# Hybrid decoder trunk: x with channels on partitions, and stationary weights with 256 moving columns in the down, output and o blocks

## The reference, cut to what matters

```python
for l in range(2):
    x = x + 0.5 * swiglu(rms_norm(x, g1), w_gate, w_up, w_down)     # q = 0, 4
    z = rms_norm(x, g2) @ w_in                                      # q = 1, 5
    x = x + concat([diff_attention(z), conformer_conv(z), short_conv(z)]) @ w_out
    x = x + cross_attention(rms_norm(x, g3), rms_norm(mem, gm)) @ xa_wo   # q = 2, 6
    x = x + 0.5 * swiglu(rms_norm(x, g4), w_gate, w_up, w_down)     # q = 3, 7
return rms_norm(x, final_norm)
# rms_norm(x, g) = x * rsqrt(mean(x * x over channels) + 1e-6) * g
# swiglu(h, wg, wu, wd) = (silu(h @ wg) * (h @ wu)) @ wd
```

## Time and profile before

| | |
|---|---|
| median of 3 runs | 1141.22 us |
| profiled execution, its own time | 1141.1 us |
| its span | 1139.3 us |
| instructions | 15680 |
| PE products | 6180 |
| weight splits on ACT, on DVE | 260 x 1475 ns, 260 x 1746 ns |
| read from HBM | 208.85 MB, 184 GB/s over the span |

### The profile page before, as it was taken

One profiled execution on the slowest core, in us unless ns is written; L12 is line 12 of the kernel. 1 busy time (PEld: TensorE's weight loads), 2 busy tenths in 40 slices (PEclk: granted clock), 3 DMA queues, 4 the chain that ended last, 5 costly groups with the idle time before them and its releaser, 6 DMA issues.

```text
span 1139.3 us, 15680 instructions
## 1 busy us (share of the span) xinstructions
PE 1131.4 (99%) x6180; PEld 976.9 (86%) x6180; DVE 857.4 (75%) x1164; ACT 647.1 (57%) x937; POOL 21.8 (2%) x63
## 2 busy tenths in 40 slices
PE   9999999999999999999999999999999999999997
PEld 8888888888889888888888888888888898888886
DVE  7877676899967686766777676669998676866765
ACT  6555556547755554544565555464577556645454
POOL 1000000000000000000000000000000000000000
PEclk9999999999999999999999999999999999999999
DMA  7966654644444366555547655544545444666561
GB/s 265 327 202 188 218 186 147 221 149 165 170 159 172 111 224 217 164 201 199 186 151 255 219 161 205 192 165 168 186 148 204 166 146 125 210 190 216 183 200 43
DMA packets 66266, 210.92 MB, mean 185 GB/s; under 512 B 5009, under 2 KB 24209, under 8 KB 61073
## 3 DMA queue, kind: packets, MB, share of 16 engines
q1 hardware_dynamic: 65216, 209.26, 54.0%
q10 hardware_dynamic: 976, 0.66, 0.2%
HBM read 208.85 MB, written 1.05 MB: 184 GB/s over the span
## 4 chain that ended last, share of the span: by engine, by line
PE 94%; DVE 4%; DVEq 1%; ACT 0%; issue 0%
PE G L1720 28%; PE G L1729 14%; PE D L1567 10%; PE D L1565 10%; PE D L1566 10%; PE G L1660 3%; PE G L1565 3%; PE G L1567 3%; PE G L1566 3%; PE D L1660 2%; DVE w_lo L1006 2%; PE G L1669 1%; DVE acc L1215 1%; PE D L1669 1%; PE D L1632 1%; DVEq L1217 1%
## 5 line engine op out<-in xcount | busy, mean ns | idle before, releaser
L1006 DVE TENSOR_TENSOR w_lo<-w_raw,w_hi 128x2048 fp32r<-128x2048 f32 (+3 forms) x260 | 452.6, 1746 | 54.8 <-ACT w_hi L595 54.0
L595 ACT ACTIVATE w_hi<-w_raw 128x2048 fp32r<-128x2048 f32 (+3 forms) x260 | 381.1, 1475 | 35.2 <-PE D L1567 17.0
L1720 PE MATMUL G<-a,w_hi 128*128 128x512 f32 x1406 | 346.3, 391 | 0.1
L1720 PEld LDWEIGHTS G<-a,w_hi 128*128 128x128 f32 x1406 | 256.1, 188 | 48.6 <-issue 1.1
L1729 PEld LDWEIGHTS G<-a,w_lo 128*128 128x128 f32 x1406 | 175.4, 188 | 8.6
L1729 PE MATMUL G<-a,w_lo 128*128 128x256 f32 x1406 | 177.5, 277 | 0.0
L1111 DVE TENSOR_TENSOR zqk<-G,zqk 128x512 f32<-128x512 f32 x88 | 60.8, 691 | 127.3 <-ACT zqk L674 123.3
L1565 PE MATMUL D<-w_hi,hT_hi 128*128 128x512 f32 x352 | 137.2, 390 | 0.0
L1567 PE MATMUL D<-w_hi,hT_lo 128*128 128x512 f32 x352 | 137.0, 389 | 0.0
L1566 PE MATMUL D<-w_lo,hT_hi 128*128 128x512 f32 x352 | 136.9, 389 | 0.0
L674 ACT ACTIVATE zqk<-G 128x512 f32<-128x512 f32 x88 | 52.2, 593 | 143.1 <-PE G L1729 143.1
(11 more groups left out here) (261 smaller groups left out, 1282.5 us busy)
## 6 DMA issues: line engine op xcount, KB each, us to landing
w_raw<-w_dram SPq DMA_DIRECT2D x120, 1024.0 KB, 5.0
w_raw<-w_dram SPq DMA_DIRECT2D x143, 512.0 KB, 5.3
m_raw<-memT_dram SPq DMA_DIRECT2D x2, 1024.0 KB, 8.8
w_raw<-w_dram SPq DMA_DIRECT2D x6, 256.0 KB, 6.5
w_raw<-w_dram SPq DMA_DIRECT2D x8, 128.0 KB, 3.8
vx<-mem_dram SPq DMA_DIRECT2D x1, 1024.0 KB, 10.8
x<-x_dram SPq DMA_DIRECT2D x2, 256.0 KB, 5.7
gbc<-fin_dram SPq DMA_DIRECT2D x1, 512.0 KB, 6.6
```

The source lines that it names most:

```text
L595: A(w_hi[:, part(i)], w_raw[:, part(i)], ACT.Copy).then_inc(s_hi, 1)
L1006: V.tensor_tensor(w_lo[:, part_lo(i)], w_raw[:, part(i)], w_hi[:, part(i)].bitcast(F32), ALU.subtract).then_inc(s_lo, 1)
L1720: last = M(banks[b], whi[:, at:at + P], both, start=k == 0 and not low_first, stop=k == KD - 1 and low_first, skip_group_check=low_first)
```

## The change

x is kept with channels on partitions ([128, 8, 256]), so that it needs no transposes ahead of a norm; the first norm's transposes stay, and their result is copied from PSUM to x by ACT. Down blocks (but those of the last FFN), `out` and `o` take the weights as stationary operand, 128 output channels at a time, and move 256 tokens: 24 products of 256 columns where there were 12 of 512. In FFNs the down pair of the odd chunks 5 to 19 stands between the chunk's low and high products; in the last FFN (`rows`) products and order stay as they were, and x is added in PSUM by 16 float32 products with 2·identity, so the final norm reads PSUM (with eps times 4). The sum of squares over channels is now over partitions: ACT squares, DVE adds (`channel_squares`), PE sums over partitions by two float32 products of one column, ACT copies the result for POOL. rinv_broadcast moves to the middle of chunk 2. The last block's banks are updated one by one (s_bank). Sizes and paddings of a, b, hT, m, kx and vx in memory change, and LINE goes from 128 to 64 elements.

```diff
+OFF = 48
+TURN = 16
...
-LINE = 128
+LINE = 64
...
-        x = sb("x", [P, TT, D])
-        a = sb("a", [P, KD, 2, T], F32R)
+        x = sb("x", [P, KD, T])
+        a_room = sb("a", [P, 2 * KD * T + OFF], F32R)
...
+        a, a_hi, a_lo = activations(0)
+        b, b_hi, b_lo = activations(OFF)
+        hT_room = sb("hT", [P, 2 * SLOTS_H * T + TURN], F32R)
...
+        hT_hi, hT_lo = hidden_places(0)
+        rows_hT = hidden_places(TURN)
...
-        hT_hi = sb("hT_hi", [P, SLOTS_H, T], F32R)
-        hT_lo = sb("hT_lo", [P, SLOTS_H, T], F32R)
+        sb("line_const", [P, 32])
...
-                squares(q, 1)
-                a_hi_part(q, range(4, 8))
+                to = norm_place(q)[0]
+                def high(j):
+                    act.wait_ge(s_xup, 4 * (q - 1) + j + 1)
+                    for k in (2 * j, 2 * j + 1):
+                        A(to[:, k, :], x[:, k, :], ACT.Copy, scale=gain(NORMS[q % 4], k)).then_inc(s_ahi, 1)
+                def squares(j):
+                    A(squared[j // 2][:, j % 2, :], x[:, 2 * j:2 * j + 2, :].rearrange("p k t -> p (k t)"), ACT.Square,
+                      scale=D ** -0.5).then_inc(s_sq, 1)
+                high(0)
+                high(1)
+                squares(0)
+                high(2)
+                squares(1)
+                high(3)
+                squares(2)
+                squares(3)
+            def mean_squares(q):
+                act.wait_ge(s_stat, q)
+                A(mean_sq[:, :], STAT_BANKS[q % 4][:, 0:TT], ACT.Copy).then_inc(s_ssq, 1)
+            def copy_first_x(banks):
+                act.wait_ge(s_alo, KD)
+                for j in banks:
+                    A(x[:, j::4, :], pair(DB[j]), ACT.Copy).then_inc(s_xcopy, 1)
...
                     norm_start(4 * l + 3 * f)
                     split(l, stage, ("gu", 2, 0, 8))
                     split(l, stage, ("gu", 3, 0, 8))
+                    mean_squares(4 * l + 3 * f)
                     copy_tail(l, f, 0)
                     broadcast(l, f)
...
+            def low_part(q, k):
+                hi, lo = norm_place(q)
+                dve.wait_ge(s_ahi, 8 * q + k + 1)
+                V.scalar_tensor_tensor(lo[:, k, :], x[:, k, :] if q else first_x(k), gain(NORMS[q % 4], k),
+                                       hi[:, k, :].bitcast(F32), ALU.mult, ALU.subtract).then_inc(s_alo, 1)
+            def x_update(q, j):
+                if j < 3:
+                    dve.wait_ge(s_bank, 3 * q + j + 1)
+                else:
+                    dve.wait_ge(s_blk, last_of(q // 4, LAST_STAGES[q % 4]) + 1)
+                xs = x[:, 2 * j:2 * j + 2, :]
+                V.scalar_tensor_tensor(xs, pair(DB[j]), FACTORS[q % 4], xs, ALU.mult, ALU.add).then_inc(s_xup, 1)
             def norm_lo(q):
-                a_lo_part(q, range(0, 2))
-                second_half(q - 1)
-                a_lo_part(q, range(2, 8))
+                x_update(q - 1, 1)
+                for k in range(0, 2):
+                    low_part(q, k)
+                x_update(q - 1, 2)
+                for k in range(2, 4):
+                    low_part(q, k)
+                x_update(q - 1, 3)
+                for k in range(4, 8):
+                    low_part(q, k)
+            def channel_squares(q):
+                dve.wait_ge(s_sq, 4 * q)
+                V.tensor_tensor(v_sb[:, :, :], v_sb[:, :, :], gbc[:, :, :], ALU.add)
+                dve.drain()
+                V.tensor_tensor(v_sb[:, 1, :], v_sb[:, 0, :], v_sb[:, 1, :], ALU.add)
+                dve.drain()
+                V.tensor_tensor(channel_sum, v_sb[:, 1, 0:T], v_sb[:, 1, T:], ALU.add).then_inc(s_chsum, 1)
...
                 else:
                     norm_lo(4 * l + 3 * f)
+                    channel_squares(4 * l + 3 * f)
+                    split(l, stage, ("gu", 2, 0, 8))
+                    if 4 * l + 3 * f == 4 * L - 1:
+                        twice_identity()
                     rinv_diag(l, f)
-                    split(l, stage, ("gu", 2, 0, 8))
                     pair_sum(l, f, 0)
                     split(l, stage, ("gu", 3, 0, 8))
                     pair_scale(l, f, 0)
...
-                return V.tensor_tensor(y[:, t, w], x[:, t, w], fing[:, w], ALU.mult)
+                dve.wait_ge(s_sqr, 2 * t + n + 1)
+                return V.tensor_tensor(y[:, t, w], DB[2 * n + t][:, :], fing[:, w], ALU.mult)
...
+            def channel_products(d, hi, lo, whi, wlo, n, k, start, stop):
+                w = slice(n * D + d * P, n * D + (d + 1) * P)
+                M(channels(d), whi[:, w], hi[:, k, :], start=start and d % 2 == 0, stop=False, skip_group_check=True)
+                M(channels(d), whi[:, w], lo[:, k, :], start=False, stop=False, skip_group_check=True)
+                return M(channels(d), wlo[:, w], hi[:, k, :], start=False, stop=stop, skip_group_check=True)
...
+            def last_down(q, hi, lo, ks):
+                whi, wlo = weights(last_of(q // 4, LAST_STAGES[q % 4]))
+                for d in range(KD):
+                    for n, k in enumerate(ks):
+                        last = channel_products(d, hi, lo, whi, wlo, n, k, False, n == 1)
+                    if d in (1, 3, 5):
+                        last.then_inc(s_bank, 1)
                 last.then_inc(s_blk, 1)
...
+            def residual_by_token():
+                pe.wait_ge(s_twice, 1)
+                pe.wait_ge(s_ssq, 4 * L)
+                for k in range(KD):
+                    for t in range(TT):
+                        M(DB[2 * (k // 4) + t][:, k % 4 * P:(k % 4 + 1) * P], x[:, k, tok(t)], twice,
+                          start=k % 4 == 0, stop=False, skip_group_check=True)
...
+            def mean_squares(q):
+                pe.wait_ge(s_chsum, q)
+                for t in range(TT):
+                    last = M(STAT_BANKS[q % 4][:, t:t + 1], channel_sum[:, tok(t)], ones[:, 0:1], start=t == 0, stop=True,
+                             skip_group_check=True)
+                last.then_inc(s_stat, 1)
...
                     for k in range(0, KD, 2):
-                        if k == 2:
-                            second_transposes(q)
+                        if k == 6:
+                            mean_squares(q)
...
+                def down_chunk(c, done):
                     pe.wait_ge(s_hlo, chunk(l, f, c))
-                def down_chunk(c):
-                    hidden_ready(c)
-                    down(l, stage, ("down", c), hT_hi, hT_lo, (c % SLOTS_H,), c == 0)
+                    if (q, c) == (0, 0):
+                        pe.wait_ge(s_xcopy, 4)
+                    if rows:
+                        token_down(l, stage, ("down", c), *rows_hT, c % SLOTS_H)
+                    else:
+                        down(l, stage, ("down", c), hT_hi, hT_lo, (c % SLOTS_H,), c == 0, done=done)
+                def down_pair(c, done=1):
+                    down_chunk(c, done)
+                    down_chunk(c + 1, done)
                 for c in range(2, STEPS):
                     pe.wait_ge(s_sum, chunk(l, f, c - 2))
-                    for ks in late_parts(l, f, c):
-                        gate_up(l, f, c, range(*ks), low_first=ks[0] == 2 if (q, c) == (0, 2) else c % 2 == 1)
-                        if (q, c, ks) == (0, 2, (0, 2)):
-                            rinv_broadcast()
-                    if c % 2 and c < STEPS - 2:
-                        down_chunk(c - 3)
-                        down_chunk(c - 2)
-                down_chunk(STEPS - 4)
-                down_chunk(STEPS - 3)
-                hidden_ready(LAST)
+                    early = c % 2 and 3 < c < STEPS - 2 and not rows
+                    if c % 2 == 0:
+                        for ks in late_parts(l, f, c):
+                            gate_up(l, f, c, range(*ks), low_first=ks[0] == 2 if (q, c) == (0, 2) else False,
+                                    middle=rinv_broadcast if q and c == 2 else None)
+                            if (q, c, ks) == (0, 2, (0, 2)):
+                                rinv_broadcast()
+                    else:
+                        for ks in late_parts(l, f, c):
+                            gate_up(l, f, c, range(*ks), low_first=True, between=(lambda: down_pair(c - 3, 0)) if early else None)
+                    if c == 3 and rows:
+                        residual_by_token()
+                    if c % 2 and c < STEPS - 2 and not early:
+                        down_pair(c - 3)
+                down_pair(STEPS - 4)
+                pe.wait_ge(s_hlo, chunk(l, f, LAST))
                 ks = ((STEPS - 2) % SLOTS_H, LAST % SLOTS_H)
-                if q < 4 * L - 1:
+                if not rows:
                     last_down(q, hT_hi, hT_lo, ks)
                     return
                 whi, wlo = weights(last_of(l, stage))
                 for t, at, end in ENDS:
-                    c = at // N
                     for n, k in enumerate(ks):
-                        w = slice(n * D + at, n * D + end)
```

(54 more changed lines are left out.)

264 lines of the change are left out of this document (128 added, 136 removed).

## The result

The changed kernel takes 1146.66 us (median of 6 runs, 1146.26 to 1146.93), the kernel before 1140.74 in the runs beside it: ratio 1.0049, 95% interval 1.0036 to 1.0062. It is slower by half a per cent, where the forecast was 1138.0, a gain of 3. The profiled execution took 1146.93, its span is 1145.2.

The account below looks back on a forecast made before the run. PE, busy 99%, was taken to bound the kernel. Gains of 13.2 us less costs of 10.2 gave net 3.0 us off the profiled 1141.1, say 1138.0 us; range 1134 to 1145.5.

Parts of the forecast that it names:

- part 1: Down, out and o: 1176 products become 2352 at 113.3 ns, some at 117.5; costs 2.0 us plus 0.3 for row changes.
- Rival B: Slower: 256-column products with changing weights cost 117.5 or 119.8 ns wherever they stand; 1146 or 1151 us; chance 0.11.
- rival A: Faster: nothing slow behind 512-column products and no wait for pair_sum; 3.8 us more gained, 1134.3 us; chance 0.15.
- Rival E: Each product costs something beside its columns; 1176 added ones cost 2.6 us, 1140.6, no change; chance 0.03.
- part 2: Seven norms: two blocks of 8 transposes each go, 0.87 us per block, 12.2 us gained over 14 blocks.
- part of 3: PE's added float32 work: mean_squares in seven norms costs 2.1 us, residual_by_token between FFN blocks 3.6 us.
- part 6: Ends and cross attention: start 0.4 us late, end 0.5 gained, the 64-byte distance in cross gains 0.5.
- part 4: Norm's serial path into an FFN: PE waits 0.6 us for pair_sum, 1.8 over three FFNs; mixer and cross 0.
- part 5: Steady FFN pairs: low weights of the odd block are ready 0.5 us before PE needs them; cost 0.
- Rival C: Slower: the steady pairs' 0.5 us cover is missing, PE waits for low weights; 1145 at 0.3 per pair; chance 0.08.

Follow-up runs that it names:

- p7: Changed kernel with the first two high products of the odd chunk put between its 16 low products and the early downs; 1141.53 us.
- p8: p5 with all places of 64 and 0 modulo 128 exchanged, for moving and stationary operands; 1151.0 us.
- p11: Kernel before the change, with even chunks in plain order: 16 high, then 16 low products, without the inserted 2 low and 2 high; 1145.36 us.
- p5: Changed kernel with hT and b at 0 modulo 128 and both w_hi and w_lo of the turned blocks at 64; 1141.37 us.
- p4: Changed kernel with a at 64 modulo 128 and no SHIFT, giving low products the places of the turned ones; 1145.8 us.
- p3: Changed kernel with two channel blocks of different banks taking turns in most down, out and o blocks, places in memory unchanged; 1146.9 us.
- p9: p5 with mean_squares earlier and, at c = 21 and c = 3, two down products ahead of the odd chunk's last two high ones; 1139.89 us.
- p12: p9 with DVE's low split of the next stage's fourth block moved behind the third update of x; 1138.80 us.
- p2: Changed kernel with hT and b at 0 modulo 128, w_hi and the turned blocks' w_lo at 64; 1157.7 us.

## Why the prediction was wrong, step by step

- **Turned products (part 1), the step that failed.** The prediction said: "all three new products have the 64-byte distance. So I take 113.3 as the ground rate", and "the pairs at c = 5 to 19 follow 30 low products, where the rate is 113.3". Both facts about the places hold. The conclusion doesn't: an equal distance was taken to be enough for the low row's 113.3 to hold in the downs behind it, though every fast row that had been seen lay at (0, 64). p7, p8 and p11 show that the rate hangs on the products before, p5 and p4 that downs keep a low row's 113.3 when their places are that row's own. In the changed kernel they are exchanged, (0, 64) to (64, 0), and 2203 of 2352 turned products ran between 116 and 122 ns. The term measured 9.1 in place of 2.3 us. Its bound, "all 2352, 9.9 us", was right and was then left out of the range.
- **Rival B** had the size ("At 117.5 everywhere ... 1146") and the wrong reason: neither a price of the product nor the triple's order (p3). What spoke against it, the row of 30 at 113.3, was one half of the truth. The sentence "16 products held 117.5 to the last", written against rival A, was the other half: a carried-over rate. So B's 1146 came near by luck of the size, not by its mechanism.
- **Rival E.** The Trainium skill's "TensorE: Matmul & The Clock Gate" (Back-to-back issue gap) gives an isolated warm product N/2.4 + 2.5 ns, by which two halves would cost 2.5 ns more than a whole, an estimate. The traces don't agree: two halves cost 0 ns more (5.44 us for 48 in p5 and for 24 before) or 9 (5.65 in the changed kernel), so there is no one surcharge.
- **Transposes and residual (part 2 and part of 3)** came as worked out: 11.1 and 1.2 of late starts behind them against 12.2, and 3.49 with 0.09 behind it against 3.6. **mean_squares** did not come cheaper by its single column: three of its four passes take 0.11 us, like those of 128 columns. It is 0.36 and 0.09 of late start against 0.3, so 3.2 us for seven against 2.1.
- **The 64-byte distance in cross attention (part 6)** brought 0.3 of the 0.5 us: the 96 score products (`S`) took 11.2 us before and after, the 96 of `pv` 11.9 and then 11.6. So here too the distance alone did not bring 113.3.
- **The serial path into an FFN (part 4)**: 0.57 against 0.6 us. Timeline of DVE and PE at the end of layer 0:

```profile
583.13 0.48 DVE L1180 TENSOR_SCALAR hT<-const,rinv 128x128 fp32r<-128x128 f32 x2 [1.32 <-POOL rinv L576]
583.69 0.61 DVE L1183 SCALAR_TENSOR_TENSOR hT<-const,rinv,hT 128x128 fp32r<-128x128 f32 x2
584.22 0.68 DVE L1190 TENSOR_TENSOR zqk<-G,zqk 128x512 f32<-128x512 f32 x1
```

```profile
583.57 1.09 PE L1818 MATMUL G<-a,w_hi 128*128 128x512 f32 x4
584.96 2.11 PE L1818 MATMUL G<-a,w_hi 128*128 128x512 f32 x8 [0.29 <-DVE zqk L1190]
```

  The copy (581.81), the diagonal (583.13 to 584.30) and pair_sum (to 584.90) stand 3 us behind the times of the prediction's working and in its order, as the head itself begins 3 us later, at 572.86. The mixer of layer 0 waits 0.4 us more than before ahead of its first scores; there I had taken 0.
- **Cover of the steady pairs (part 5)** held: PE waits for no w_lo in a pair, and the period's 0.24 us more are the 48 products' (5.65 - 5.44) and 0.03 of row changes. Rival C did not happen.
- **The end (part 6)**: 0.9 gained against 0.5.

With 9.1 in place of 2.3 the sum of the prediction is 1144.9. The profiled execution took 1146.93; most of the other 2 us are mean_squares (1.1) and the mixer's wait (0.4).

## What to carry to other kernels

A rate read from rows is the rate behind what stood in front of them: before a new row is priced with it, look for one row that follows the same kind of neighbour, and if there is none, carry both rates as bounds for the whole count into the range (here 0 to 10.4 us), and don't price only the part that seems exposed. The rate of one pair isn't yet that of all: p8's 24 pairs go both ways. A gain in the last block before a dependent stage can be given back there (0.2 us of wait more at each of three heads in p9) until the other engine's order is changed too (p12).

## What the runs showed of the hardware

- A row of 256-column products runs at 113.3 or at 117.8 ns per product, with the same code and the same addresses (p8). The rate is handed on: where the places stay the same, downs keep their low row's rate, fast (p5, p4) or slow (half the pairs of p8). It stays slow for 32 products (p11) and for 96 (o of layer 1).
- Behind two 512-column products a row of 256-column ones was fast in all 41 rows of 30 of the kernel before and in the downs of all 24 early pairs of p7, but slow in the low rows of 12 of p8's 24 pairs and of 23 of p2's. Rows turned slow where (0, 64) was followed by (64, 0) without a product between (the changed kernel, 24 pairs). What in the engine this is, and what decides how a row starts, wasn't settled.
- 512-column products: sums of the 1598 high ones by their places, in us: (0, 0) 368.2, (0, 64) 371.4 (p2), (64, 64) 374.1 (p8), (64, 0) 375.1 (p4). Against (0, 0) that is 2.0, 3.7 and 4.3 ns each; the rows beside them changed as well in these runs.
- A float32 pass with one moving column costs 0.11 us, as much as one with 128 (mean_squares and residual_by_token in the changed kernel).
